# Two unused tensors that move the weight ring and the later operands to other addresses modulo 512

## The reference

```python
x = x + concat([y_pool, y_attn]) @ w_out
x = x + conv_ffn(rmsnorm(x, ffn_norm_g), w_up, conv_w, conv_b, w_down)
h = x + (g_a * (y_a @ w_branch_a) + g_b * (y_b @ w_branch_b)) @ w_out
h = h + (silu(hn @ w_gate) * (hn @ w_up)) @ w_down
return rmsnorm(h, final_norm)
```

## Time and profile before

| | |
|---|---|
| Median of 3 runs | 2447.98 us (2447.17 to 2448.62) |
| The profiled execution | 2449.52 us, of which the span from first to last instruction is 2447.7 us |
| TensorE matmul busy | 2433.5 us, 99% of the span |
| TensorE weight load busy | 2018.0 us, 82% |
| VectorE / ScalarE busy | 1320.5 us, 54% / 1181.1 us, 48% |
| Matmuls | 11152 |
| Weights read | 446 MB; the DMA queue of the weights takes 60.4% of the 16 engines |

### The profile page before, as it was taken

One profiled execution on the slowest core, in us unless ns is written; L12 is line 12 of the kernel. 1 busy time (PEld: TensorE's weight loads), 2 busy tenths in 40 slices (PEclk: granted clock), 3 DMA queues, 4 the chain that ended last, 5 costly groups with the idle time before them and its releaser, 6 DMA issues.

```text
span 2447.7 us, 29829 instructions
## 1 busy us (share of the span) xinstructions
PE 2433.5 (99%) x11152; PEld 2018.0 (82%) x11152; DVE 1320.5 (54%) x1480; ACT 1181.1 (48%) x1489; POOL 57.1 (2%) x97
## 2 busy tenths in 40 slices
PE   9999999999999999999999999999999999999998
PEld 7788888888888888888888888888888888888886
DVE  5675455666666655445454554665545445454443
ACT  5544445555555544445455544544444444444443
POOL 0000000000000000001120000000000000000000
PEclk9999999999999999999999999999999999999999
DMA  7665456666666655556655556556666666666564
GB/s 239 180 177 168 147 183 187 188 182 185 187 185 184 185 189 189 189 189 182 188 166 172 162 163 181 187 183 188 187 190 187 190 189 188 189 189 205 192 193 140
DMA packets 240904, 449.38 MB, mean 184 GB/s; under 512 B 20084, under 2 KB 26964, under 8 KB 240688
## 3 DMA queue, kind: packets, MB, share of 16 engines
q1 hardware_dynamic: 239952, 445.83, 60.4%
q0 software_dynamic: 624, 2.24, 0.3%
q10 hardware_dynamic: 240, 0.11, 0.0%
HBM read 446.02 MB, written 2.10 MB: 183 GB/s over the span
## 4 chain that ended last, share of the span: by engine, by line
PE 70%; issue 29%; DMA 0%; DVE 0%; SPq 0%; ACT 0%; POOLq 0%; POOL 0%; DVEq 0%; ACTq 0%
PE acc L551 22%; PE acc L553 22%; PE acc L552 21%; PE bank L542 2%; PE bank L704 1%; PE bank L732 0%; PE bank L762 0%; PE bank L681 0%; DMA x_res<-in_x 0%; PE bank L733 0%; PE bank L707 0%; PE bank L747 0%; PE acc L580 0%; PE acc L582 0%; PE acc L581 0%
## 5 line engine op out<-in xcount | busy, mean ns | idle before, releaser
L1266 DVE TENSOR_TENSOR w_lo<-w_raw,w_hi 128x1024 fp32r<-128x1024 f32 (+1 forms) x843 | 1030.1, 1222 | 1084.3 <-ACT w_hi L941 1083.1
L941 ACT ACTIVATE w_hi<-w_raw 128x1024 fp32r<-128x1024 f32 (+1 forms) x843 | 890.0, 1056 | 1222.1 <-PE acc L553 1217.3
L551 PE MATMUL acc<-w_hi,xT_hi 128*128 128x512 f32 x2236 | 878.7, 393 | 0.0
L553 PE MATMUL acc<-w_hi,xT_lo 128*128 128x512 f32 x2236 | 868.7, 388 | 0.0
L552 PE MATMUL acc<-w_lo,xT_hi 128*128 128x512 f32 x2236 | 867.7, 388 | 0.0
L553 PEld LDWEIGHTS acc<-w_hi,xT_lo 128*128 128x128 f32 x2236 | 419.7, 188 | 87.3
L551 PEld LDWEIGHTS acc<-w_hi,xT_hi 128*128 128x128 f32 x2236 | 419.9, 188 | 84.7 <-issue 1.3
L552 PEld LDWEIGHTS acc<-w_lo,xT_hi 128*128 128x128 f32 x2236 | 420.2, 188 | 83.2
L551 PE MATMUL acc<-w_hi,f_hi 128*128 128x512 f32 x704 | 277.2, 394 | 0.0
L553 PE MATMUL acc<-w_hi,f_lo 128*128 128x512 f32 x704 | 276.1, 392 | 0.0
L552 PE MATMUL acc<-w_lo,f_hi 128*128 128x512 f32 x704 | 273.6, 389 | 0.0
(11 more groups left out here) (203 smaller groups left out, 1184.2 us busy)
## 6 DMA issues: line engine op xcount, KB each, us to landing
w_raw<-in_w_up SPq DMA_DIRECT2D x264, 512.0 KB, 3.7
w_raw<-in_w_in SPq DMA_DIRECT2D x199, 512.0 KB, 3.7
w_raw<-in_w_down SPq DMA_DIRECT2D x176, 512.0 KB, 3.9
w_raw<-in_w_gate SPq DMA_DIRECT2D x88, 512.0 KB, 3.7
w_raw<-in_w_out SPq DMA_DIRECT2D x64, 512.0 KB, 3.7
w_raw<-in_w_branch_a SPq DMA_DIRECT2D x16, 512.0 KB, 3.9
w_raw<-in_w_branch_b SPq DMA_DIRECT2D x16, 512.0 KB, 3.8
w_raw<-in_w_in SPq DMA_DIRECT2D x10, 320.0 KB, 3.1
```

Of the source, the lines that this page charges most:

```text
L551: pe.matmul(o, l, w_hi[:, slot, k, 0:width], start=start, stop=False)
L553: last = pe.matmul(o, m, w_hi[:, slot, k, 0:width], start=False, stop=stop)
L941: act.activation(in_slot(w_hi, slot, width), in_slot(w_raw, slot, width), ACT.Copy).then_inc(w_split_hi, 1)
L1266: dve.tensor_tensor(in_slot(w_lo, slot, width), in_slot(w_raw, slot, width), in_slot(w_hi, slot, width).bitcast(F32), ALU.subtract).then_i ...
```

## The change

Two tensors that nothing reads or writes are added. `place_ring` has 96 floats, 384 bytes a partition, between `xT_lo` and `w_raw`. `place_inner` has 48 floats, 192 bytes, before `y_hi`. No instruction is added, removed or reordered.

```diff
         xT_hi, xT_lo = sb("xT_hi", [P, KT, S], F32R), sb("xT_lo", [P, KT, S], F32R)
+        sb("place_ring", [P, 96])
         w_raw = sb("w_raw", [P, RING, KC, CW])
...
         negmax, psum_, pinv = sb("negmax", [P, 4]), sb("p_sum", [P, 4]), sb("p_inv", [P, 4])
 
+        sb("place_inner", [P, 48])
         with ExitStack() as r:
             y_hi, y_lo = sb("y_hi", [P, KT, S], F32R, r), sb("y_lo", [P, KT, S], F32R, r)
```

## The result

The changed kernel takes 2492.93 us (median of 4 runs, 2492.4 to 2493.62) against 2447.57 us (4 runs, 2446.97 to 2448.62) for the kernel before on the same chip: ratio 1.0187, 95% interval 1.0174 to 1.0199. It is 45.4 us slower, where 7.5 us less were forecast. Its profiled execution took 2492.79 us, the span of it 2491.0.

What follows compares the result with a forecast made beforehand. TensorE's matmul pace was taken as the bound; 1128 triples saving 6.7 ns each gave -7.5 us, all other terms 0, so 2447.98 us became 2440.5 us, with a range of 2437 to 2463.

Steps and rivals of the forecast that it cites:

- what bounds the kernel: Whole kernel: TensorE's matmuls, busy 99% of the span at full clock; only what alters TensorE's pace can alter the time.
- the two paces of before: Matmul triples: 680.0 ns with x stationary, level with the moving operand; 686.6 to 686.8 with f, y, m, at -64.
- the price of -64: Triples with y, m, cq, ckv and f stationary: 6.7 ns each for lying 64 below the moving operand; 1128 triples, 7.5 us.
- +128 as good as 0, or at worst as bad as -64: All triples after the change: as good gives 7.5 us off; as bad costs x's 2236 triples 15.0 us more.
- settling after breaks: Slower first matmuls after transposes in the x stage, some 90 re-entries: no change taken, plus or minus 3.9 us at most.
- rival 1: +128 is a bad place and x's triples pay up to 15.0 us, no gain elsewhere: 2463 us; chance 0.25.
- the 80-column group: Matmuls with 80 stationary columns, distances 0 to 192: k = 2 may carry 3 to 13 ns, bounding +128 between free and bad.
- the reading by absolute address: Stationary operands starting at 128 or 192 modulo 256 are fast, at 0 or 64 slow; so +128 is free.
- rival 4: At +128 the two reads never meet, each matmul falls to 215 ns: 116 us off, 2332 us; chance 0.04.
- the floor's account: Fastest matmul of 512 columns, 226.7 ns: 213.3 of stream plus 32 cycles, one for each 16 bytes of stationary operand.
- Rival 3: Placement has no effect; the 6.7 ns come from the stage and not the address: 2448.0 us; chance 0.08.
- 0 for the splits, the landing of the weights and the transposes: VectorE and ScalarE splits and weight DMAs stay hidden under TensorE, transposes show no cost of placement: 0 us.

Runs made afterwards that it cites:

- all_moved: Kernel before plus 384 unused bytes ahead of `x_res`: every tensor moves, no distance between operands changes; 2446.69 us against 2446.99, ratio 0.9999.
- ring_only: Kernel before plus `place_ring` alone (384 bytes): x at distance +128, the other stationary operands still at -64; 2482.12 us against 2446.99, ratio 1.0144.
- inner_only: Kernel before plus `place_inner` alone (192 bytes): x stays at distance 0, the other stationary operands at +128; 2459.49 us against 2446.99, ratio 1.0051.
- bench: Whole computation left out: TensorE alone, 84 matmuls in a row at each of 24 distances, then other widths and moving places; one execution, 664.86 us.
- level: Kernel before plus `place_inner` of 64 bytes alone: distance 0 for every stationary operand; 2440.70 us against 2446.99, ratio 0.9974.
- bench_fine: Whole computation left out: TensorE alone, 60 matmuls at each distance from 0 to 252 in 4-byte steps, then 32 to 128 stationary columns; never under 544 cycles.
- raw_only: Kernel before with `w_raw` alone moved to 0 modulo 512, all else in place modulo 512; 2446.64 us against 2446.99, ratio 0.9999.

## Why the prediction was wrong, and where it was right

**Right: what bounds the kernel, and the two paces of before.** Only TensorE's pace moved, with the other engines' busy times and the clock as they were. The distance of the two reads sets that pace: `all_moved`, `ring_only` and `inner_only` show it in the kernel and `bench` without one. 680.0 and 686.7 ns came back for 0 and -64 in every kernel that had them, but for the 48 matmuls with cqT in `ring_only`.

**Right: the price of -64.** The forecast was made of 1128 triples at 6.7 ns. `level` does that and nothing else, and gives 6.3 to 7.0 us.

**Wrong: the price of +128, in the step "+128 as good as 0, or at worst as bad as -64".** The first was chosen and the second taken as the bound; it is neither. +128 costs 17.1 ns a triple over 0 and 10.4 over -64. By the counts: of the 2236 triples with x 32 are only 320 columns wide, where `bench` shows no effect, and 2204 x 17.1 is 37.7 us; 1128 x 10.4 is 11.7 us; 49.4 together. Before, x's triples already had a mean of 681.3 ns with the settling after breaks, and after it 697.4, so 16.1 of the 17.1 ns came on top: 35.5 + 11.7 = 47.2 us, where 45.4 were measured (42.6 to 48.7). The forecast was 2440.5, its sum with the true term 2447.6 + 47.2 = 2494.8 us, and the time is 2492.93.

**Why the bound failed.** It was the price of the one other place that the trace held. That was a single point of an unknown curve, and by `bench` the cheapest of all but level. Nothing at 512 columns in the trace excluded a dearer place. The range ended at 2463, the time of rival 1 with that price; rival 1 had the right mechanism and the right sign, its point of decision (2.2 ns) was passed almost eight times over, and only its size was too small.

**Right in the reading, wrong in the use: the 80-column group.** "3 to 13 ns for the three of k = 2" was taken as a bound on +128 for 512 columns. After the change that group's distances are the old ones shifted by 128: 128, 192, 0 and 64 modulo 256 for k = 0 to 3, then the same again. The timeline of TensorE in the changed kernel, every second k of the second chunk, and the transpose behind them:

```profile
36.73 0.28 PE L582 MATMUL acc<-xT_hi,w_hi 128*80 128x256 f32 x1
...
37.44 0.28 PE L582 MATMUL acc<-xT_hi,w_hi 128*80 128x256 f32 x1
...
38.13 0.28 PE L582 MATMUL acc<-xT_hi,w_hi 128*80 128x256 f32 x1
...
38.83 0.28 PE L582 MATMUL acc<-xT_hi,w_hi 128*80 128x256 f32 x1
...
39.52 0.27 PE L544 MATMUL bank<-ident,stage 128*128 128x128 f32 x1
```

The pairs of k take 0.71, 0.69, 0.70 and 0.69 us, where the earlier trace rows have 0.69, 0.70, 0.69 and 0.71: the dear pair has moved with the distance. The starts in both traces, to the nanosecond and once the group has settled, give 345 ns from a k at 0 to the next, 345 or 346 at 64, 350 at 128 and 352 or 353 at 192. So the price was there and was read rightly: 12 ns for six matmuls, of which some 5 at +128 and 7 or 8 at -64. In this shape +128 is the cheaper of the two; with 128 stationary and 512 moving columns it is the dearer. The failure lies in carrying it from one shape to the other, and `bench` shows how little that can be done: at 256 moving and 128 stationary columns 0 is the dearest of the three tried.

**Wrong: the reading by absolute address**, which tipped the choice towards free. In `all_moved` the stationary operands with x start at 0, a slow place by that reading, and those with f at 448 (192 modulo 256), a fast one, and both keep their pace.

**Wrong: rival 4's and the floor's account, one cycle for each 16 bytes.** It fitted two shapes and had two numbers to fit. The four widths of `bench_fine` refute it. That the floor doesn't go was right all the same: 544 cycles is the least late mean in the 92 rows of 60 or 84 matmuls of 512 columns that the two benches have with 128 stationary ones.

**Rival 3, no effect of placement**, is out by `level` and `ring_only` alone, 0.9974 and 1.0144. The Trainium skill gives it too, in "TensorE: Matmul & The Clock Gate", Part 2, by two independent read ports; the measurements decide against that for this type and width, with 226.7 to 234.3 ns a matmul by placement and no other engine at work. Its sentence in "SBUF — State Buffer", two separate sides, that PE never waits on anyone speaks of other engines. So read it agrees with the runs, since the paces of `bench` without other engines are those of the kernel; it just says nothing of TensorE's own two reads, and the prediction took it too far.

**Right: 0 for the splits, the landing of the weights and the transposes.** `raw_only` is 0.9999 (0.999 to 1.0009), and the passes over the ring last 1226 and 1060 ns after the change. The settling after breaks was put at nothing too. It shrank: the mean with x stood 1.3 ns above the steady 680.0 before, and 0.2 above 697.2 after, which takes about 2 us off the loss.

What stays open: why +128 is dearer than -64, what the order of the distances comes from, what decides which pattern a stretch falls into, and what counts below 32 bytes. That it is the load of the stationary operand that meets the stream is argued from the fact that the difference of their two places counts. No run keeps one stationary operand for several matmuls without loading it anew, so that it is the load is not shown by itself.

## What to carry to other kernels

Where TensorE is the bound with fp32r matmuls of 512 moving and 128 stationary columns, each with its own load, put both operands at the same place modulo 256 bytes (both on multiples of 32) and measure; it costs a few unused bytes and was worth 0.26% here, while a wrong distance cost 1.9%. When a trace holds two points of an unknown curve, the price of the worse one is not a bound for a third. And a price read from one shape must be measured again before it is used for another: here the order of the distances changed with the shape.

## What the hardware showed that was not expected

- A matmul of 512 columns in fp32r with a load for each takes 226.7, 228.9, 232.4, 233.3 or 234.3 ns by the distance modulo 256 in steps of 32 bytes, with TensorE alone at work; the kernel as a whole goes from 2440.4 to 2492.9 us by it.
- The paces settle in patterns that repeat after a whole number of matmuls. At 0 each takes 544 cycles. At -64 three take 1648: 232, 226 and 229 ns. At +128 seven take 3904: 230, 232, 241, 232, 231, 232 and 228 ns. All three sums are multiples of 16 cycles. One distance can have two patterns: at +128 two of the twelve long stretches with x in the changed kernel, and three of twelve in `ring_only`, settle at 699.9 ns a triple and not at 697.2. The first matmuls after a break are slower: 228.0 ns in the mean of the first row of `bench`, 226.7 later.
- The order of the distances depends on the width: with 128 stationary columns, at 256 moving ones 0 costs 288 cycles and -64 282.7, at 320 columns there is no difference (352), at 448 columns 486.8 and 479.8.
- 32 stationary columns are no cheaper than 128 at full rate (556 against 544 cycles).
- 4 bytes can decide: 227.8 ns at 156, 234.2 at 160 and 238.0 at 164.
